# State-space stage of a two-block kernel: decays issued two chunks ahead, GpSimd's operand ahead of the scaled input, last state left out

## What is computed

```python
xbc = silu(causal_dwconv(xbc_raw, conv_w, conv_b)); xs, bm, cm = split(xbc)
dt = softplus(dt_raw + dt_bias); adt = dt * -exp(a_log)
a_cs = cumsum(adt)                                    # within a chunk
lmat = exp(where(causal, a_cs[l] - a_cs[s], -inf))    # decays, 128 x 128 per head
cb = einsum('bclgn,bcsgn->bcgls', cc, bc)             # G, per group
y_diag = einsum(cb * lmat, xs * dt)
states = einsum(bc, exp(a_cs[-1] - a_cs), xs * dt)    # one per chunk
y_off = einsum(cc, prev_states, exp(a_cs))            # state left by the chunks before
y = y_diag + y_off + xs * d_skip
gated = rms_norm(y * silu(z)) * norm_g                # per group of 512 columns
```

## Time and profile before

| what | value |
|---|---|
| median of three runs | 2502.8 us (2501.65 to 2503.9) |
| the profiled execution | 2503.09 us |
| its span, first to last instruction | 2500.9 us |
| PE busy | 2330.7 us, 93% |
| DVE busy | 1268.9 us, 51% |
| ACT busy | 780.6 us, 31% |
| POOL busy | 139.1 us, 6% |
| mean granted clock of PE | 0.959 |

### The profile page before, as it was taken

The page is one execution under the profiler, slowest core; times in us unless marked ns, Lnnn a source line. Parts: engine busy times, 40 slices in busy tenths (PEclk is TensorE's granted clock), DMA queues, the critical chain, the costliest instruction groups (busy, mean ns, idle before and its releaser), DMA issues. The chain is left out here.

```text
span 2500.9 us, 26283 instructions
## 1 busy us (share of the span) xinstructions
PE 2330.7 (93%) x10746; PEld 1743.6 (70%) x10746; DVE 1268.9 (51%) x1867; ACT 780.6 (31%) x1237; POOL 139.1 (6%) x127
## 2 busy tenths in 40 slices
PE   6999998879999999999999999978789999898999
PEld 3445853567788888788888678965567977443887
DVE  3779539375644334244443475137746186664310
ACT  3101112532333322244322442334334232344210
POOL 0000000200000000000000000035300000021000
PEclk9999988959999999999999999999999999798999
DMA  7541029004233333234333211000131110102332
GB/s 259 161 125 33 1 67 325 22 18 155 82 100 93 101 107 93 80 101 127 93 110 93 83 52 52 18 1 26 46 85 65 38 34 17 68 18 69 104 85 59
DMA packets 272911, 204.15 MB, mean 82 GB/s; under 512 B 17650, under 2 KB 252458, under 8 KB 271864
## 3 DMA queue, kind: packets, MB, share of 16 engines
q1 hardware_dynamic: 257772, 186.31, 24.6%
q0 software_dynamic: 3136, 10.25, 1.2%
q10 hardware_dynamic: 11884, 5.91, 0.9%
HBM read 175.26 MB, written 26.01 MB: 80 GB/s over the span
## 5 line engine op out<-in xcount | busy, mean ns | idle before, releaser
L1944 PE MATMUL bk_in<-h_part,w_part 128*128 128x512 f32 x2112 | 484.6, 391 | 4.5 <-DVE w_part L2172 4.3
L1944 PEld LDWEIGHTS bk_in<-h_part,w_part 128*128 128x128 f32 x2112 | 397.2, 188 | 91.1 <-issue 5.7
L2035 ACT ACTIVATE w_part<-w_raw 128x1024 fp32r<-128x1024 f32 (+1 forms) x136 | 154.5, 1136 | 531.4 <-PE bk_in L1944 310.5
L2172 DVE TENSOR_TENSOR w_part<-w_raw,w_part 128x1024 fp32r<-128x1024 f32 (+1 forms) x136 | 179.3, 1319 | 210.1 <-ACT w_part L2035 210.0
L1944 PE MATMUL bk_out<-hid_part,w_part 128*128 128x512 f32 x1056 | 240.3, 389 | 0.0
L1944 PEld LDWEIGHTS bk_out<-hid_part,w_part 128*128 128x128 f32 x1056 | 198.2, 188 | 41.6 <-issue 0.5
L991 PE MATMUL fr_ps<-arena,work 128*128 128x512 f32 x384 | 168.7, 601 | 5.1 <-DMA work<-in_w_in 5.1
L3696 PE MATMUL fo_ps<-fo_hi,fo_part 128*128 128x512 f32 x512 | 161.8, 394 | 10.9 <-DVE fo_lo L3740 10.9
L2509 PE MATMUL bk_in<-h_part,sj_part 128*128 128x512 f32 x576 | 135.4, 396 | 6.8 <-DVE h_part L2260 5.7
L991 PEld LDWEIGHTS fr_ps<-arena,work 128*128 128x128 f32 x384 | 73.6, 193 | 96.6 <-issue 90.8
L2942 PE MATMUL aj_ps<-h_part,aj_part 128*128 128x512 f32 x576 | 137.8, 400 | 0.0
(11 more groups left out here) (567 smaller groups left out, 3330.0 us busy)
## 6 DMA issues: line engine op xcount, KB each, us to landing
w_raw<-in_w_ffn_in SPq DMA_DIRECT2D x88, 512.0 KB, 3.8
work<-in_w_mod SPq DMA_DIRECT2D x24, 1024.0 KB, 8.1
w_raw<-in_w_ffn_out SPq DMA_DIRECT2D x32, 704.0 KB, 4.6
work<-in_w_in SPq DMA_DIRECT2D x25, 512.0 KB, 3.8
w_raw<-in_w_in SPq DMA_DIRECT2D x20, 512.0 KB, 3.8
w_raw<-in_w_out SPq DMA_DIRECT2D x16, 512.0 KB, 4.1
work<-in_w_out SPq DMA_DIRECT2D x8, 1024.0 KB, 6.9
kept_mix<-work SPq DMA_DIRECT2D x12, 512.0 KB, 2.6
```

Source lines behind the costliest of these rows:

```text
L1944: mm = pe.matmul(bank, w_part[:, n % 2, a, k, :], moving(b, k), start=(first and k == 0 and j == 0), stop=(last and k == kt - 1 and j == 2))
L2035: nc.scalar.activation(w_part[:, n % 2, 0, 0:kt, :], w_raw[:, n % 2, 0:kt, :], ACT.Copy)\
L2172: nc.vector.tensor_tensor(w_part[:, n % 2, 1, 0:kt, :], w_raw[:, n % 2, 0:kt, :], f32(w_part[:, n % 2, 0, 0:kt, :]), ALU.subtract).then_in ...
```

## The change

- GpSimd: R(0) is made in the stage before, once four half-tiles are turned (`gpsimd(pool)`), over the two tiles that this sets free. In the stage the order is skip(c), xdt(c), R(c+1), xds(c); there is no xds(7).
- PE: no wait for constants. Decays(1) come behind Y(0), and decays(c+2) behind st(c), ahead of turn(c-1). There is no st(7).
- ACT: exponentials(c+2) ahead of squares(c); out(c-1) behind squares(c), then root(c).
- DVE: the constants move to the stage before. products(c+1) and out(c-2) by turns ahead of mean(c-1); norm(c-1) behind kept. diagonals become a tensor_tensor with `ms` broadcast, mean a scalar_tensor_tensor with a tile of EPS. kept(7) and upd(7) go, and with them a memset (L3596) that only raised a semaphore.

The diff, cut to its core:

```diff
@@ stage_back, gpsimd
+                next_part.gpsimd(pool)
@@ SsdProjection
+        S.ss_ident = rounded(nc, S, "ss_ident", YY0 + 2048, P)
+        S.ss_early = rounded(nc, S, "ss_early", YY0 + 2048 + 128, P)
+        self.R = A.view(XC0, SSD_H, P)
...
+    def gpsimd(self, pool):
+        s, S, V = self.s, self.S, self.V
+        pool.wait_ge(s.adt, 1)
+        pool.wait_ge(s.turned, 4)
+        pool.tensor_tensor(self.R, S.t_le.unsqueeze(1).broadcast_to([P, SSD_H, P]),
+                           V.adt[:, 0, :].unsqueeze(2).broadcast_to([P, SSD_H, P]), ALU.mult)
...
         dve.wait_ge(s.done, 2 * self.N_SC + 4 * NT)
+        nc.vector.tensor_copy(S.ss_ident[:, :], S.ident)
+        nc.vector.tensor_scalar(S.ss_early[:, :], S.t_le, -1.0, 1e30, ALU.add, ALU.mult)
         for n, (m, h) in enumerate(self.jobs):
@@ stage_ssd, gpsimd
                 for c in range(NC):
-                    if c:
-                        pool.wait_ge(s.seg, 4 * c)
-                    pool.tensor_tensor(R, S.t_le.unsqueeze(1).broadcast_to([P, SSD_H, P]),
-                                       adt[:, c, :].unsqueeze(2).broadcast_to([P, SSD_H, P]), ALU.mult)\
-                        .then_inc(s.R, 1)
                     if c >= 2:
                         pool.wait_ge(s.sq, 2 * c - 2)
                     pool.tensor_tensor(hd(yy[c % 2]), hd(xt[:, c, :]), bh(dsk), ALU.mult).then_inc(s.skip, 1)
                     pool.wait_ge(s.skip, c + 1)
                     pool.tensor_tensor(hd(xt[:, c, :]), hd(xt[:, c, :]), bh(dt[:, c, :]), ALU.mult).then_inc(s.xdt, 1)
...
+                    if c + 1 < NC:
+                        pool.wait_ge(s.seg, 4 * c + 4)
+                        pool.tensor_tensor(R, S.t_le.unsqueeze(1).broadcast_to([P, SSD_H, P]),
+                                           adt[:, c + 1, :].unsqueeze(2).broadcast_to([P, SSD_H, P]), ALU.mult)\
+                            .then_inc(s.R, 1)
+                        pool.wait_ge(s.xdt, c + 1)
+                        if c:
+                            pool.wait_ge(s.st_mm, c)
+                        pool.tensor_tensor(hd(xds), hd(xt[:, c, :]), bh(ds[:, c, :]), ALU.mult).then_inc(s.xds, 1)
@@ tensor
-                pe.wait_ge(s.consts, 2)
                 decays(0)
                 for c in range(NC):
                     tok = slice(c * P, (c + 1) * P)
-                    if c + 1 < NC:
-                        decays(c + 1)
...
+                    if c == 0:
+                        decays(1)
+                    if c + 1 < NC:
+                        pe.wait_ge(s.xds, c + 1)
+                        if c:
+                            pe.wait_ge(s.added, c)
...
+                    if c + 2 < NC:
+                        decays(c + 2)
                     if c:
                         pe.wait_ge(s.y_ok, c + 1)
                         turn(c - 1)
@@ scalar
                 decays(0)
+                decays(1)
                 for c in range(NC):
-                    if c >= 2:
-                        out(c - 2)
-                    if c + 1 < NC:
-                        decays(c + 1)
+                    if c + 2 < NC:
+                        decays(c + 2)
...
+                    if 0 < c < NC - 1:
+                        out(c - 1)
+                    root(c)
@@ vector
-                nc.vector.tensor_copy(ident_r[:, :], S.ident).then_inc(s.consts, 1)
-                nc.vector.tensor_scalar(early_r[:, :], S.t_le, -1.0, 1e30, ALU.add, ALU.mult).then_inc(s.consts, 1)
+                nc.vector.memset(eps, EPS).then_inc(s.consts, 1)
...
-                        nc.vector.tensor_scalar(diag[:, g, :], S.ident, ms[:, c, g:g + 1], None, ALU.mult)\
+                        nc.vector.tensor_tensor(diag[:, g, :], S.ident, ms[:, c, g:g + 1].broadcast_to([P, P]), ALU.mult)\
                             .then_inc(s.diag, 1)
...
-                    nc.vector.tensor_scalar(ms[:, c, :], ms[:, c, :], 1.0 / HALF, EPS, ALU.mult, ALU.add).then_inc(s.ms, 1)
+                    nc.vector.scalar_tensor_tensor(out=ms[:, c, :], in0=ms[:, c, :], scalar=1.0 / HALF, in1=eps,
+                                                   op0=ALU.mult, op1=ALU.add).then_inc(s.ms, 1)
```

More of the change, by code:

```diff
@@ L3402, in stage_ssd @@
     at = YY0 + 2048
-    ident_r = rounded(nc, S, "ss_ident", at, P)
-    early_r = rounded(nc, S, "ss_early", at + 128, P)
+    ident_r, early_r = S.ss_ident, S.ss_early
     diag = A.view(at + 256, 2, P)
     ms = A.view(M_SMALL + 256, NC, 2)
+    eps = A.view(M_SMALL + 272, 2)
     assert at + 512 <= SM0
@@ L3440, in _ @@
                     pool.tensor_tensor(hd(xt[:, c, :]), hd(xt[:, c, :]), bh(dt[:, c, :]), ALU.mult).then_inc(s.xdt, 1)
-                    pool.wait_ge(s.xdt, c + 1)
-                    if c:
-                        pool.wait_ge(s.st_mm, c)
-                    pool.tensor_tensor(hd(xds), hd(xt[:, c, :]), bh(ds[:, c, :]), ALU.mult).then_inc(s.xds, 1)
+                    if c + 1 < NC:
[7 more added lines that the diff above has]
+                        pool.tensor_tensor(hd(xds), hd(xt[:, c, :]), bh(ds[:, c, :]), ALU.mult).then_inc(s.xds, 1)
             @block.tensor
@@ L3495, in _ @@
                     mm.then_inc(s.Y, 1)
-                    pe.wait_ge(s.xds, c + 1)
-                    if c:
-                        pe.wait_ge(s.added, c)
-                    for g in range(SSD_G):
-                        mm = pe.matmul(po[:, g, :], bt[:, c, g * P:(g + 1) * P], xds[:, g * HALF:(g + 1) * HALF],
-                                       start=True, stop=True)
-                    mm.then_inc(s.st_mm, 1)
+                    if c == 0:
+                        decays(1)
+                    if c + 1 < NC:
+                        pe.wait_ge(s.xds, c + 1)
+                        if c:
+                            pe.wait_ge(s.added, c)
+                        for g in range(SSD_G):
+                            mm = pe.matmul(po[:, g, :], bt[:, c, g * P:(g + 1) * P], xds[:, g * HALF:(g + 1) * HALF],
+                                           start=True, stop=True)
+                        mm.then_inc(s.st_mm, 1)
+                    if c + 2 < NC:
+                        decays(c + 2)
                     if c:
@@ L3580, in _ @@
                     y = yy[c % 2]
+                    if 0 < c < NC - 1:
+                        products(c + 1)
                     if c >= 2:
                         out(c - 2)
-                    if c + 1 < NC:
-                        products(c + 1)
+                    if c:
+                        mean(c - 1)
                     dve.wait_ge(s.skip, c + 1)
                     if c:
-                        norm(c - 1)
                         dve.wait_ge(s.offs, c)
@@ L3592, in _ @@
                         nc.vector.tensor_tensor(y, y, flat(po[:, :, :]), ALU.add).then_inc(s.added, 1)
-                        nc.vector.tensor_tensor(hd(st), hd(st), bh(et[:, c, :]), ALU.mult).then_inc(s.kept, 1)
+                        if c + 1 < NC:
+                            nc.vector.tensor_tensor(hd(st), hd(st), bh(et[:, c, :]), ALU.mult).then_inc(s.kept, 1)
+                        norm(c - 1)
                         dve.wait_ge(s.added, c)
-                    else:
-                        nc.vector.memset(V.ww[:, 0, 0:1], 0.0).then_inc(s.kept, 1)
                     dve.wait_ge(s.Y, c + 1)
@@ L3600, in _ @@
                     nc.vector.tensor_tensor(zs[:, c, :], flat(pd[:, :, :]), zs[:, c, :], ALU.mult).then_inc(s.y_ok, 1)
-                    dve.wait_ge(s.st_mm, c + 1)
-                    if c:
-                        dve.wait_ge(s.kept, c + 1)
-                        k = nc.vector.tensor_tensor(st, st, flat(po[:, :, :]), ALU.add)
-                    else:
-                        k = nc.vector.tensor_copy(st, flat(po[:, :, :]))
-                    k.then_inc(s.upd, 1)
-                    mean(c)
+                    if c == 0:
+                        products(1)
+                    if c + 1 < NC:
+                        dve.wait_ge(s.st_mm, c + 1)
+                        if c:
+                            dve.wait_ge(s.kept, c)
+                            k = nc.vector.tensor_tensor(st, st, flat(po[:, :, :]), ALU.add)
+                        else:
+                            k = nc.vector.tensor_copy(st, flat(po[:, :, :]))
+                        k.then_inc(s.upd, 1)
+                mean(NC - 1)
                 norm(NC - 1)
```

9 lines of the change are left out of this document (6 added, 3 removed).

## The result

The changed kernel takes 2480.2 us (median of 4, 2479.97 to 2481.78) against 2503.05 for the kernel before on the same chip (median of 4): ratio 0.991, 95% interval 0.990 to 0.992. Predicted were 2481.0 and a range of 2469 to 2487. Its profiled execution took 2481.78 us, 2479.8 of it span.

The account below looks back on a forecast made before the run. No engine was full; a ring of waits, 17.30 us per chunk, was taken to set the pace. Terms 17.2 + 8.0 - 3.5 = 21.7 gained, from 2503.09 to 2481.4, less 0.3 for the median: 2481, range 2469 to 2487.

Parts of the forecast that it names:

- Entry, cost 0: Constants and first R moved to the stage before cost 0, at most 0.6 us; decays(0) start at 1657.3.
- First chunks, walked: Start of the stage, up to decays(3): 17.2 us gained, including 1.4 allowed for a clock drop.
- Without the mean's wait the ring is 14.1: Settled chunks: a ring through GpSimd, TensorE and ScalarE takes 14.1 us, TensorE's own instructions about 13.8.
- mean waits, 15.3 a chunk: Four settled chunks: VectorE's mean ends with xdt, 1.7 late, making the ring 15.3 instead of 17.30; 8.0 us gained.
- kept and the diagonals lie beside the ring: Settled chunks: kept waits 1.2 for R, the first diagonal 1.7 for xds, neither on the ring that sets the pace.
- rival C: Settled chunks: waits of kept and diagonals pile up, y_ok becomes last; 16.8 a chunk, 2487 us; chance 0.09.
- forecast A: Settled chunks: the mean waits, 15.3 a chunk; own range 2478 to 2485 us; chance 0.67.
- The end, 3.5 lost: From decays(7) to the next stage's first memset: 36.8 us instead of 33.3, 3.5 lost.
- Later stages move as a block: Stages behind this one: they move as a block; no separate term for them in the sum.
- B: Settled chunks: the mean does not wait, each chunk is 1.3 shorter; 8.8 more gained, 2472.5 us; chance 0.19.
- D: Settled chunks: VectorE and GpSimd take turns, 22.0 a chunk; slower, 2515 us; chance 0.02.
- E: Decays two ahead are pinned by two buffers or by products; only the entry's 5.6 gained, 2497.5 us; chance 0.03.

Follow-up runs that it names:

- e3: The changed kernel with the two constants and the first R put back at the start of the stage: 2490.81 us, ratio 0.995 to the kernel before.
- e4: The kernel before with only the constants and the first R moved to the stage before: 2496.86 us, ratio 0.998 to the kernel before.
- e7: The changed kernel with the last chunk's xds, state product, kept and update computed again, unread: 2479.42 us, ratio 0.991 to the kernel before.
- e8: The changed kernel with the squares' unread outputs thrown into used columns of xc, so skip waits for the sum only: 2473.43 us, ratio 0.988.
- e9: e8 and e1 together on the changed kernel (squares thrown elsewhere, mean on ScalarE): 2468.93 us, ratio 0.986 to the kernel before.
- e1: The changed kernel with the mean's division and constant folded into ScalarE's root, no mean on VectorE: 2481.64 us, ratio 0.992 to the kernel before.
- e11: e10 and e1 together on the changed kernel (norm ahead of kept, mean on ScalarE): 2476.82 us, ratio 0.989 to the kernel before.
- e10: The changed kernel with VectorE issuing norm(c-1) ahead of kept(c) instead of behind it: 2476.65 us, ratio 0.989 to the kernel before.
- e2: The changed kernel with mean and diagonals as tensor_scalar again, in their new places: 2480.76 us, ratio 0.991 to the kernel before.
- e12: e9 with the last chunk's state, kept and scaled input computed again, unread: 2469.01 us, ratio 0.986 to the kernel before.
- e5: The kernel before with the entry edit and GpSimd's new order, TensorE still one chunk ahead: 2493.61 us, ratio 0.996 to the kernel before.
- e6: The changed kernel with GpSimd's old order, the next R behind xds: 2509.73 us, ratio 1.002 to the kernel before.

## Why the prediction was right, and where only its sum was

1. *Entry, cost 0.* Right. decays(0) start at 1658.73, which is 1657.24 on the clock of before (predicted 1657.3), at granted clock 1.00. In the stage before, where VectorE was idle, the two constants take 0.23 and 0.22:

```profile
1648.57 0.23 DVE L2665 CAST ss_ident<-arena 128x128 fp32r<-128x128 f32 x1 [43.02 <-PE bk_in L2535]
1648.71 0.22 DVE L2666 TENSOR_SCALAR ss_early<-arena 128x128 fp32r<-128x128 f32 x1
```

instead of 3.68 and 1.94 in the earlier trace rows. e3 puts the entry at 7.4 us inside the stage, e4 at 6.6 in the time (2503.47 for the kernel before in that run).

2. *First chunks, walked.* Right to 0.1 in the sum (decays(3) at 1691.49 against 1691.4), by luck in the clock: two deviations cancel. decays(2) came at 1674.78 as walked, but the low clock fell on them and not on decays(3), and then on decays(3) as well, where it counts for the loop. e7, whose program is the same up to there, shows the walk itself: decays(3) at 1689.80 on the clock of before, against 1690.0, and one low stretch behind. The walk had looked at the gap ahead of decays(3) alone and taken 1.7 us as a gap that keeps the clock at 1.00; in the changed kernel it fell behind 1.57, ahead of decays(2).

3. *Without the mean's wait the ring is 14.1, TensorE's work 13.8.* The second number is right: 13.98 in e8, 13.59 in e9. The first was never reached, for the reason in point 4.

4. *mean waits, 15.3 a chunk; kept and the diagonals lie beside the ring.* This is the step that failed, though its term came out (8.1 for 8.0), and that it did is luck. The mean waits when it meets GpSimd, 1.42 to 1.51 long (predicted about 1.9), but it did so in three chunks only, once for skip and twice for xdt; in the rest it took 0.15, and taking it away changed nothing (e1, e11). What carries the settled chunks is the clause put aside, "kept waits for R (1.2) and holds xds up; the first diagonal waits for xds (1.7). Both lie beside this ring". kept waited up to 3.1 (4.30 for 1.22), since its VectorE queue brings it soon after R's start and not at R's end. Then come the diagonals, 1.5 to 1.7 late, the sum, y_ok and the squares, which release skip: 14.5, or 15.1 in the cycles where the last exponential, behind TensorE's queue, held ScalarE longer than y_ok did. That last leg (decays, exponentials, squares) is the prediction's, without a wait of the mean that counts. Moving norm ahead took 3.6 us off in the median (e10), freeing skip 6.8 (e8). So the mechanism was in good part rival C's (y_ok last), at forecast A's size. The signs set down beforehand say the same: A's are there (kept 4.10 and ending after R, decays(3) near 1691), and so is C's, y_ok releasing TensorE's turn at 1743.95. C priced it at 16.8 because I added its waits to the mean's, one behind the other; in the queue one wait absorbs the other. 1754.09 - 1692.98 also holds one low stretch: the last exponential of decays(3) starts 6.33 behind their first matmul, that of decays(4) 4.66, and the squares follow it at once. By these rows the four chunks would have gained 1.7 more at full clock, 9.8 and not 8.1; this is an estimate, as every run with this order had the low clock over decays(3).

That two-input form waits is what the Trainium skill, "SBUF — State Buffer", section "Who interferes with whom", says of an instruction with two SBUF inputs beside a GpSimd instruction that reads SBUF; mean, kept and diagonals all agree with it (1.51 for 0.15, 4.30 for 1.22, 2.00 for 0.49). The same section has the one that comes second block, whichever engine it is. The trace agrees there too. GpSimd's R took 4.59 behind a kept that had started before it, 1.0 more than its 3.61, where the prediction's walk had put 1.2 for this meeting:

```profile
1686.93 2.52 DVE L3617 TENSOR_TENSOR work<-work 128x1024 f32<-128x1024 f32 x1
...
1688.34 4.59 POOL L3451 TENSOR_TENSOR work<-arena,work 128x2048 f32<-128x2048 f32 x1
```

xds took 2.89 for 1.90 at 1708.61.

5. *The end, 3.5 lost.* 3.2 measured. The walk had turn(6) at full clock; it ran at 0.54, 1.6 slower, so the other steps were 1.8 shorter than walked. That this came out is luck too: with the same end in the program it was 38.81 us in e1 and 38.38 in e2, where both turns ran low, and not 36.56. "All beside the last chain" is right for the time: putting the last state back costs nothing (e7, e12), so leaving it out gained nothing, and the products left out had also kept TensorE from idling.

*Later stages move as a block.* Only to a few us. Over the kernel before, the changed one and the twelve here, what lies behind this stage took 688.0 to 692.4 us in the profiled executions, the longest two (e3, e12) at a granted clock of 0.95 over all of it, the other twelve at 0.96. What lies ahead of it, up to the first output transpose, took 1645.8 to 1648.7, also with the same code. A difference of up to 3 or 4 us between two single executions can thus come from stages that nobody edited. That is the size of the effects that e3 and e12 were made for. That the phase in which the next stage is entered decides it is my reading; no run moved the phase alone.

*Rivals.* B (14.1, the mean slips in) is out: e1 had no mean on VectorE and stayed at 15.1. D (the engines in series, 22 a chunk) is out by the spacing of 15.3, and E too: the order did what it says, and e5 and e6 show that it takes both of its halves. A rival that the prediction did not name is TensorE's queue, with Y behind VectorE's out: it makes the 15.1 of every second cycle, and no run moved it alone.

## What to carry to other kernels

When two engines share a port, look at every instruction in the later one's queue and not at the one that waited in the old trace: a wait removed ahead of another wait is worth nothing, and shows its price only once the other is gone (the mean: nothing in e1 and e11, 3.0 us of the stage in e9). Free the resource that makes the cycle (in e8 the place into which the squares are thrown, 6.8 us) before changing forms or orders of the instructions that suffer in it. Treat a gain of one or two us from the clock in one stage as unproven until the whole program shows it.

## What the runs showed of the hardware that was not expected

- A long VectorE instruction held by GpSimd ends about its own length after GpSimd's: kept 1.08 behind R. Two short ones in a row can each meet another GpSimd instruction if GpSimd has its next one queued (pair 5.08 and 5.41), and only one does if it has a gap (1.39).
- It works in both directions: R 4.59 for 3.61, xds 2.89 for 1.90.
- In these traces a low clock did not need a long gap. The clock fell behind 1.57 us of idle time at 1676.27 in the changed kernel and stayed at 1.00 behind the same 1.57 at 1676.29 in e7; at the end it was low behind a gap of 2.65 ahead of turn(6) in the changed kernel and in all eight of its variants without the last state, and stayed at 1.00 behind 1.50 in the two with it.
